# A causal convolution computed by parity of tokens, group sums in float32r, and the first tokens laid out by part

## The chip, the cores and the metric

The kernel runs on one core of a Trainium2 chip. The metric is the device time of one execution in microseconds, the median of several runs.

## The reference, cut to what matters

One decoder layer, 2048 tokens of 1024 channels, all in float32. This case touches the first of its stages (phase A): the normalisation of x, the projection `w_in`, and the two causal convolutions over tokens, above all the wide one:

```python
u = conv_val * jax.nn.sigmoid(conv_gate)
u = causal_depthwise_conv(u, conv_w[layer], conv_b[layer])      # width 31, 512 channels
uf = u.astype(jnp.float32).reshape(B, S, N_CONV_GROUPS, CONV_GROUP_DIM)
mu_c = jnp.mean(uf, axis=-1, keepdims=True)                     # over 128 channels of a group
var_c = jnp.mean(jnp.square(uf - mu_c), axis=-1, keepdims=True)
uf = ((uf - mu_c) * lax.rsqrt(var_c + EPS)).reshape(B, S, D_CONV)
uf = uf * conv_norm_w[layer] + conv_norm_b[layer]
y_conv = jax.nn.silu(uf)
```

Queries and keys pass a convolution of width 4 and a silu. Behind it come the mLSTM, the output projection, two norms and the MLP; none of them is changed.

## The kernel before, in words

Channels lie on partitions and tokens along the free axis. Every large product is made of three float32r matmuls, high by high, high by low and low by high part of both operands. A high part is a rounding copy on ScalarE (ACT), a low part a subtraction on VectorE (DVE).

Phase A goes in 96 **slots** (SLOTS). A slot is one PSUM bank of output, 24 matmuls of 128x512 or 48 of half the width (kinds v and o). PE, ACT and DVE each have their own program, written slot by slot: for every slot `s` ACT evacuates the bank when PE has ended the slot (`evacuate`, semaphore proj), and then does the other steps that belong to `s`, in the order of the code; DVE does the same for its own. Nothing is reordered at run time, so a step that waits holds up everything that stands behind it on its engine.

The wide convolution comes in 8 **units** (4 groups of 128 channels, 2 halves of 1024 tokens). `glu` writes a unit's input into `u_buf`, a ring of three. On DVE a unit is 30 steps of `tap`: taps 2 to 30, each a multiply-add over 1024 tokens, alternately into `c_buf` and `c_odd`, and one addition of the two. Taps 0 and 1 are made on ACT by `first_tap` (into c_buf, of which there are two) and `second_tap` (into c_odd, of which there is one). `tap_plan` decides how many steps DVE does in each slot: a slot has room 100, a tap costs TAP_COST 23, a convolution of queries or keys 76, a split of weights 22. CONV_END[u] is the slot in which a unit ends. By it the norm's steps are placed: at CONV_END + 1 PE sums over channels by float32 matmuls with a matrix of ones (`group_sum`, L501), at + 2 DVE centers, at + 3 ACT squares, at + 4 PE sums again, at + 5 ACT makes the reciprocal root, at + 6 DVE multiplies, at + 7 ACT applies silu and stores the result.

The convolutions of width 4 (`first_tap_qk` on ACT L649, `convolve_qk` on DVE L852, `silu_qk` on ACT L655 with a store) stand at the slots of Q_AT: 10, 13, 15, 17, then 33, 35, 37, 39, 49, 51, 53, 55, 73, 75, 77, 79. ACT does `silu_qk` of slot s - 2 and then `first_tap_qk` of slot s, both on the one buffer `qout`, so the first tap waits until the store of the convolution before has landed.

At the start SP loads x of the first 512 tokens in two parts of 256 (`load_first`), the parameters, and the first weight tiles. PE makes warming matmuls (`warm`), then sums of squares of x in float32 (L388), while ACT and DVE square and split.

## Time and profile before

| | |
|---|---|
| time, median of 3 runs | 2086.41 us (2086.11 to 2086.6) |
| the profiled execution, time | 2085.33 us |
| its span, first to last instruction | 2083.5 us |
| granted TensorE clock, mean | 0.998 |
| PE busy | 2067.1 us (99%), 10031 matmuls |
| DVE, ACT, POOL busy | 1446.1, 912.1, 417.2 us |
| HBM traffic | 225.58 MB read, 111.21 MB written |

Durations are those of one execution by the hardware's profiler. A record's duration holds the latency of the engine too, so where instructions follow each other closely, the distance of their starts is what each takes. A bracket behind a row of a timeline gives the idle time before it and who ended it. A float32 matmul shows as two records, one for each pass.

### The profile page before, as it was taken

How to read it: one execution, taken by the hardware profiler on the slowest of the kernel's cores; microseconds unless marked ns; L12 is line 12 of the kernel's file. 1: busy time of each engine (PE TensorE's matmuls, PEld its weight loads, DVE VectorE, ACT ScalarE, POOL GpSimd, SP SyncE). 2: the span in 40 equal slices, each digit the busy share in tenths (PEclk: the TensorE clock that was granted, in tenths of full speed). 3: DMA queues.
4: the chain of work that ended last, by engine and by line, in shares of the span. 5: the costliest groups of instructions: out<-in, count | busy, mean ns of one | idle time of the engine just before them, and what ended most of it. 6: DMA issues, size and time to landing. Idle time of an engine off the chain costs nothing. (4 is left out here: it accounts for less than half of the span.)

```text
span 2083.5 us, 26901 instructions
## 1 busy us (share of the span) xinstructions
PE 2067.1 (99%) x10031; PEld 1734.2 (83%) x10031; DVE 1446.1 (69%) x1993; ACT 912.1 (44%) x1557; POOL 417.2 (20%) x252
## 2 busy tenths in 40 slices
PE   9999999999999999999999999999999999999998
PEld 8897878878788888788888888888788888888887
DVE  6897999989567777886666976666563536624285
ACT  6632434343454445754555654455331313313163
POOL 0000000000002323352332333232353134400012
PEclk9999999999999999999999999999999999999999
DMA  5121212113656875765446755545756455543376
GB/s 204 32 87 47 70 41 81 51 32 105 199 177 195 266 235 171 266 192 167 137 142 191 236 171 156 167 150 189 245 210 259 154 193 202 174 169 126 138 257 218
DMA packets 254144, 338.55 MB, mean 162 GB/s; under 512 B 11584, under 2 KB 195648, under 8 KB 240192
## 3 DMA queue, kind: packets, MB, share of 16 engines
q1 hardware_dynamic: 221376, 315.80, 45.6%
q10 hardware_dynamic: 32384, 20.98, 3.2%
q8 instruction: 81, 1.33, 0.3%
q14 instruction: 47, 0.39, 0.1%
q0 software_dynamic: 256, 0.07, 0.0%
HBM read 225.58 MB, written 111.21 MB: 162 GB/s over the span
## 5 line engine op out<-in xcount | busy, mean ns | idle before, releaser
L1978 PE MATMUL psum<-x_hi,w_hi_P 128*128 128x512 f32 x896 | 349.8, 390 | 3.8 <-DVE x_lo L1922 2.4
L2198 PE MATMUL psum<-w_hi,hid_hi 128*128 128x512 f32 x896 | 348.8, 389 | 1.9 <-DVE hid_lo L2074 1.9
L1978 PE MATMUL psum<-x_lo,w_hi_P 128*128 128x512 f32 x896 | 349.1, 390 | 0.0
L1978 PE MATMUL psum<-x_hi,w_lo_P 128*128 128x512 f32 x896 | 349.1, 390 | 0.0
L2198 PE MATMUL psum<-w_hi,hid_lo 128*128 128x512 f32 x896 | 348.6, 389 | 0.0
L2198 PE MATMUL psum<-w_lo,hid_hi 128*128 128x512 f32 x896 | 348.6, 389 | 0.0
L2074 DVE TENSOR_TENSOR hid_lo<-hid_raw,hid_hi 128x1024 fp32r<-128x1024 f32 x112 | 174.4, 1593 | 211.4 <-ACT hid_hi L2069 211.4
L1891 POOL TENSOR_TENSOR w_raw<-w_raw 128x512 f32<-128x512 f32 x128 | 184.9, 1467 | 395.3 <-DVE w_lo_P L1904 345.8
L2069 ACT ACTIVATE hid_hi<-hid_raw 128x1024 fp32r<-128x1024 f32 x112 | 112.9, 1051 | 343.4 <-DMA hid_raw<-scratch_hid 343.3
L1904 DVE TENSOR_TENSOR w_lo_P<-w_raw,w_hi_P 128x512 fp32r<-128x512 f32 x224 | 184.1, 834 | 98.1 <-ACT w_hi_P L1900 95.5
L1900 ACT ACTIVATE w_hi_P<-w_raw 128x512 fp32r<-128x512 f32 x224 | 136.0, 626 | 236.8 <-PE psum L1978 227.2
L1978 PEld LDWEIGHTS psum<-x_hi,w_hi_P 128*128 128x128 f32 x896 | 168.4, 188 | 40.4 <-issue 5.9
L2198 PEld LDWEIGHTS psum<-w_hi,hid_hi 128*128 128x128 f32 x896 | 168.2, 188 | 37.5 <-issue 2.7
L1978 PEld LDWEIGHTS psum<-x_hi,w_lo_P 128*128 128x128 f32 x896 | 168.5, 188 | 35.5
L1978 PEld LDWEIGHTS psum<-x_lo,w_hi_P 128*128 128x128 f32 x896 | 168.6, 188 | 34.7
L2198 PEld LDWEIGHTS psum<-w_hi,hid_lo 128*128 128x128 f32 x896 | 168.2, 188 | 35.0
L2198 PEld LDWEIGHTS psum<-w_lo,hid_hi 128*128 128x128 f32 x896 | 168.2, 188 | 34.9
L2030 POOL TENSOR_TENSOR w_raw<-w_raw,w_grain 128x1024 f32<-128x1024 f32 x48 | 137.9, 2888 | 224.5 <-DMA w_grain<-in_w 224.5
L841 DVE SCALAR_TENSOR_TENSOR c_buf<-u_buf,par_a,c_buf 128x1024 f32<-128x1024 f32 x120 | 153.2, 1276 | 0.0
L841 DVE SCALAR_TENSOR_TENSOR c_odd<-u_buf,par_a,c_odd 128x1024 f32<-128x1024 f32 x112 | 142.9, 1276 | 5.2 <-ACT c_odd L638 5.2
L404 PE MATMUL psum<-big_hi,w_hi 128*128 128x512 f32 (+1 forms) x288 | 109.0, 378 | 0.8 <-DVE big_lo L795 0.7
L2323 DVE TENSOR_TENSOR c<-c,psum 128x512 f32<-128x512 f32 x96 | 65.4, 681 | 61.9 <-PE psum L1978 61.9
(284 smaller groups left out, 3820.0 us busy)
## 6 DMA issues: line engine op xcount, KB each, us to landing
scratch_hid<-stage SPq DMA_DIRECT2D x224, 256.0 KB, 3.7
hid_raw<-scratch_hid SPq DMA_DIRECT2D x56, 1024.0 KB, 4.9
w_raw<-in_w SPq DMA_DIRECT2D x52, 1024.0 KB, 5.0
w_grain<-in_w SPq DMA_DIRECT2D x48, 512.0 KB, 5.3
x_raw<-scratch_h2s SPq DMA_DIRECT2D x14, 1024.0 KB, 8.4
w_raw<-in_w_in SPq DMA_DIRECT2D x22, 512.0 KB, 3.6
scratch_h2s<-h2s SPq DMA_DIRECT2D x8, 1280.0 KB, 10.1
scratch_qk<-qout ACTq DMA_DIRECT2D x16, 512.0 KB, 3.3
```

The lines of the kernel that those rows point to most:

```text
L404: mm = nc.tensor.matmul(out, a, b, start=kt == 0 and i == 0, stop=kt == KT - 1 and i == 2)
L841: nc.vector.scalar_tensor_tensor(out=out, in0=u_buf[:, u % U_RING, k:k + HALF], scalar=par[:, CONV_W + g * CW + k:CONV_W + g * CW + k + 1] ...
L1891: nc.gpsimd.tensor_tensor(raw_1(op), raw_1(a), raw_1(b), ALU.subtract).then_inc(sem["w1_t"], 1)
L1900: nc.scalar.activation(w1_hi[op][:], raw_1(op), ACT.Copy).then_inc(sem["w1_hi"], 1)
L1904: nc.vector.tensor_tensor(w1_lo[op][:], raw_1(op), w1_hi[op][:].bitcast(F32), ALU.subtract).then_inc(sem["w1_lo"], 1)
L1978: mm = nc.tensor.matmul(psum[:, bank_1(op, g), :], l, r, start=kt == 0 and i == 0, stop=kt == 3 and i == 2)
L2030: nc.gpsimd.tensor_tensor(part, part, grain[:, n % 2], alu).then_inc(sem["w2_t"], 1)
L2069: nc.scalar.activation(hid_hi[n % HID_RING][:, half_fps(h)], hid_raw[n % HID_RING][:, half_fps(h)], ACT.Copy).then_inc(sem["hid_hi"], 1)
L2074: nc.vector.tensor_tensor(hid_lo[n % HID_RING][:, half_fps(h)], hid_raw[n % HID_RING][:, half_fps(h)], hid_hi[n % HID_RING][:, half_fps(h) ...
L2198: mm = nc.tensor.matmul(psum[:, bank, :], l, r, start=f == 0 and k == 0, stop=f == NFP - 1 and k == 2)
L2323: nc.vector.tensor_tensor(out[:], a[:], ps1(op, g), ALU.add).then_inc(sem["gather"], 1)
```

## The change

1. **The convolution by parity.** `u_buf` holds the even and the odd tokens of a unit in two halves. With E and O the input's even and odd tokens, the even outputs are A + B (A: even taps on one half, B: odd taps on the other), the odd outputs are M - A' - B, where M takes sums of neighbouring inputs (`add_pairs`, step S) with sums of neighbouring weights (`add_weights`). A unit is 48 steps on about 512 elements instead of 30 on 1024: S, 15 of A, 14 of B, 15 of M, and E, T, O, which combine them. Three first taps on ACT (`first_taps` for A and B, `pair_tap` for M) replace two. A and B lie in one buffer `ab_buf`; `first_taps` stands at slot max(CONV_START - 1, glu_end, CONV_END of the unit before) and waits for that unit's T and O. A step costs STEP_COST 11.5 in the plan.
2. **The norm's sums in float32r.** ACT makes a high part of the unit (AT_HIGH) and of its square, DVE the low parts (AT_LOW, AT_SQUARE_LOW), and PE adds high and low by float32r matmuls: 8 per unit instead of 4 float32 ones. The steps stand at other slots (UNIT_AT), and the low part of a unit goes to DVE behind the taps and q/k convolution of slot CONV_END + 1.
3. **The first 512 tokens.** They lie in DRAM as `x_first`, by part; the first part comes in two DMAs by halves of channels, with w0 before them and the parameters behind them. ACT and DVE square alternate pairs, both split w0 first. 18 warming matmuls stand where 30 stood.

The silu writes tokens back in order (stride 2). The diff, cut to its core:

```diff
-DVE_TAPS = CW - 1
+EVEN, ODD = (CW + 1) // 2, CW // 2
+UH = HALF // 2
+UX = UH + EVEN
 
 
 def tiles_of(slot):
...
+AT_HIGH, AT_SUM_HIGH, AT_LOW, AT_SUM_LOW, AT_CENTER, AT_SQUARE, AT_SQUARE_LOW, AT_VAR, AT_RSTD, AT_NORM, AT_SILU = (
+    "high", "sum_high", "low", "sum_low", "center", "square", "square_low", "var", "rstd", "norm", "silu")
+UNIT_AT = {AT_HIGH: 0, AT_SUM_HIGH: 1, AT_LOW: 1, AT_SUM_LOW: 2, AT_CENTER: 2, AT_SQUARE: 3, AT_SQUARE_LOW: 3,
+           AT_VAR: 4, AT_RSTD: 5, AT_NORM: 6, AT_SILU: 7}
+LAST_UNIT_AT = {AT_HIGH: 0, AT_SUM_HIGH: 1, AT_LOW: 1, AT_SUM_LOW: 2, AT_CENTER: 2, AT_SQUARE: 2, AT_SQUARE_LOW: 2,
+                AT_VAR: 3, AT_RSTD: 3, AT_NORM: 3, AT_SILU: 3}
+LN_SUMS = 6
 FIRST_LOOP = 11
-TAP_COST = 23
+STEP_COST = 11.5
...
+WARM, WARM_MORE = 18, 8
...
+def unit_steps():
+
+    out = [("S", 0)]
+    for j in range(1, EVEN):
+        out += [("A", j)] + ([("B", j)] if j < ODD else []) + ([("M", j - 1)] if j > 1 else [])
+    return out + [("E", 0), ("M", EVEN - 1), ("T", 0), ("O", 0)]
...
-            room -= 22 * sum(out[s - AT_NORM] >= DVE_TAPS * (u + 1) > out[s - AT_NORM - 1] for u in range(N_UNITS))
-        ends = [min(i for i in range(s) if out[i] >= DVE_TAPS * (u + 1)) for u in range(n // DVE_TAPS)]
+            for at in (AT_LOW, AT_CENTER, AT_SQUARE_LOW, AT_NORM):
+                room -= 22 * sum(out[s - UNIT_AT[at]] >= N_STEPS * (u + 1) > out[s - UNIT_AT[at] - 1] for u in range(N_UNITS))
...
-        more = max(0, min(ready - n, room // TAP_COST))
+                ready = min(ready, N_STEPS * u)
+        more = max(0, min(ready - n, int(room // STEP_COST)))
...
-FIRST_TAP = [max(min(s for s in range(N_SLOTS) if TAPS[s] > DVE_TAPS * u) - 1, glu_end(u)) for u in range(N_UNITS)]
-CONV_END = [min(s for s in range(N_SLOTS) if TAPS[s] >= DVE_TAPS * (u + 1)) for u in range(N_UNITS)]
-
-SECOND_TAP = [max(FIRST_TAP[u], CONV_END[u - 1] if u else 0) for u in range(N_UNITS)]
+CONV_START = [min(s for s in range(N_SLOTS) if TAPS[s] > N_STEPS * u) for u in range(N_UNITS)]
+CONV_END = [min(s for s in range(N_SLOTS) if TAPS[s] >= N_STEPS * (u + 1)) for u in range(N_UNITS)]
+
+FIRST_TAP = [max(CONV_START[u] - 1, glu_end(u), CONV_END[u - 1] if u else 0) for u in range(N_UNITS)]
+
+PAIR_TAP = [max(FIRST_TAP[u], CONV_START[u]) for u in range(N_UNITS)]
...
+        ab_buf = sb("ab_buf", [P, 2 * UH + 1])
+        a_sum, b_sum = ab_buf[:, 0:UH + 1], ab_buf[:, UH + 1:2 * UH + 1]
...
-                sp.dma_start(big["raw"][:, :, at], dram["xt"][:, :, at]).then_inc(sem["x_in"][part], 16)
+                for half, landed in enumerate((sem["x_in"][0], sem["x_head"])) if part == 0 else ():
+                    kt = slice(half * KT // 2, (half + 1) * KT // 2)
+                    sp.dma_start(big["raw"][:, kt, at], dram["x_first"][0, :, kt]).then_inc(landed, 16)
+                if part == 1:
+                    sp.dma_start(big["raw"][:, :, at], dram["x_first"][1]).then_inc(sem["x_in"][1], 16)
...
+            load_w(0)
             load_first(0)
             sp.dma_start(par[:], dram["params_a"]).then_inc(sem["par_a"], 16)
-            load_w(0)
...
-                elif kt < KT // 2:
-                    pe.wait_ge(sem["x_sq"], kt // 2 + 1)
                 else:
-                    pe.wait_ge(sem["x_sq_dve"], (kt - KT // 2) // 2 + 1)
+                    pe.wait_ge(sem["x_sq" if kt // 2 % 2 == 0 else "x_sq_dve"], kt // 4 + 1)
...
-            def group_sum(src, b):
-                nc.tensor.matmul(psum[:, 6 + b, :], ones[:], src[:, b * TB:(b + 1) * TB],
-                                 start=True, stop=True).then_inc(sem["ln_sum"], 1)
+            def group_sum(src, b, start, stop):
+                return nc.tensor.matmul(psum[:, 6 + b, :], ones_r[:], src[:, b * TB:(b + 1) * TB], start=start, stop=stop)
...
-                for u in units_at(s, AT_MEAN):
-                    pe.wait_ge(sem["tap"], DVE_TAPS * (u + 1))
+                for u in units_at(s, AT_SUM_HIGH):
+                    pe.wait_ge(sem["ln_act"], 3 * u + 1)
                     if u == 0:
                         pe.wait_ge(sem["x_rstd"], NTB + 1)
                     else:
                         pe.wait_ge(sem["c_rstd"], 2 * u)
                     for b in range(2):
-                        group_sum(c_buf[:, u % 2], b)
+                        group_sum(high_part(u), b, True, False).then_inc(sem["ln_sum"], 1)
+                for u in units_at(s, AT_SUM_LOW):
+                    pe.wait_ge(sem["ln_dve"], 3 * u + 1)
+                    for b in range(2):
+                        group_sum(high_part(u), b, False, True).then_inc(sem["ln_sum"], 1)
                 for u in units_at(s, AT_VAR):
-                    pe.wait_ge(sem["c_sq"], u + 1)
+                    pe.wait_ge(sem["ln_act"], 3 * u + 3)
+                    pe.wait_ge(sem["ln_dve"], 3 * u + 3)
                     for b in range(2):
-                        group_sum(rstd, b)
+                        group_sum(high_part(u), b, True, False)
+                        group_sum(square_low, b, False, True).then_inc(sem["ln_sum"], 1)
...
-            def first_tap(u):
+            def first_taps(u):
                 g = u // 2
                 act.wait_ge(sem["evac"]["dve"], 2 * (u + 1))
                 act.wait_ge(sem["u_head"], u + 1)
-                if u >= 2:
-                    act.wait_ge(sem["c_out"][u % 2], 16 * (u // 2))
-                nc.scalar.activation(c_buf[:, u % 2], u_buf[:, u % U_RING, 0:HALF], ACT.Identity,
+                if u >= 1:
+                    act.wait_ge(sem["tap"], step_done(u - 1, "T"))
+                nc.scalar.activation(a_sum, u_halves(u)[:, 0, 0:UH + 1], ACT.Identity,
                                      scale=par[:, CONV_W + g * CW:CONV_W + g * CW + 1],
                                      bias=par[:, CONV_B + g:CONV_B + g + 1]).then_inc(sem["tap0"], 1)
-
-            def second_tap(u):
+                if u >= 1:
+                    act.wait_ge(sem["tap"], step_done(u - 1, "O"))
+                nc.scalar.activation(b_sum, u_halves(u)[:, 1, 0:UH], ACT.Copy,
+                                     scale=par[:, CONV_W + g * CW + 1:CONV_W + g * CW + 2]).then_inc(sem["tap0"], 1)
+
+            def pair_tap(u):
                 g = u // 2
-                if u >= 1:
-                    act.wait_ge(sem["tap"], DVE_TAPS * u)
-                nc.scalar.activation(c_odd[:], u_buf[:, u % U_RING, 1:1 + HALF], ACT.Copy,
-                                     scale=par[:, CONV_W + g * CW + 1:CONV_W + g * CW + 2]).then_inc(sem["tap0"], 1)
+                act.wait_ge(sem["tap"], step_done(u, "S"))
+                if u >= 2:
+                    act.wait_ge(sem["c_silu"], u - 1)
+                nc.scalar.activation(m_sum(u), u_pairs(u)[:, 0:UH], ACT.Identity, scale=pair_weight(g, 0),
+                                     bias=pairs[:, H * EVEN + g:H * EVEN + g + 1]).then_inc(sem["tap0"], 1)
...
+            split_w(0)
+            for q in (0, 2):
+                square_pair(q, 0)
+            split_w(1)
             act.wait_ge(sem["par_a"], 16)
...
+                for u in units_at(s, AT_HIGH):
+                    act.wait_ge(sem["tap"], step_done(u, "O"))
+                    nc.scalar.activation(high_part(u), c_buf[:, u % 2], ACT.Copy).then_inc(sem["ln_act"], 1)
                 for u in units_at(s, AT_SQUARE):
-                    act.wait_ge(sem["c_center"], u + 1)
+                    act.wait_ge(sem["ln_dve"], 3 * u + 2)
                     if u >= 1:
                         act.wait_ge(sem["c_norm"], u)
-                    nc.scalar.activation(rstd[:], c_buf[:, u % 2], ACT.Square).then_inc(sem["c_sq"], 1)
+                        act.wait_ge(sem["c_out"][(u - 1) % 2], 16 * ((u - 1) // 2 + 1))
+                    nc.scalar.activation(rstd[:], c_buf[:, u % 2], ACT.Square).then_inc(sem["ln_act"], 1)
+                    act.wait_ge(sem["ln_act"], 3 * u + 2)
+                    act.wait_ge(sem["ln_sum"], LN_SUMS * u + 4)
+                    nc.scalar.activation(high_part(u), rstd[:], ACT.Copy).then_inc(sem["ln_act"], 1)
...
+                    nc.scalar.activation(c_tokens(u)[:].rearrange("p (n a) -> p a n", a=2),
+                                         c_buf[:, u % 2].rearrange("p (a n) -> p a n", a=2), ACT.Silu,
+                                         scale=par[:, CN_W + g:CN_W + g + 1],
...
-                        first_tap(u)
-                    if SECOND_TAP[u] == s:
-                        second_tap(u)
+                        first_taps(u)
+                    if PAIR_TAP[u] == s:
+                        pair_tap(u)
...
+                at = ODD + (tb % 2) * TB // 2
                 if tb % 2 == 0 and u >= U_RING:
-                    dve.wait_ge(sem["tap"], DVE_TAPS * (u - U_RING + 1))
+                    dve.wait_ge(sem["ln_sum"], LN_SUMS * (u - U_RING + 1))
...
+                gate, val = (a.rearrange("p (n a) -> p a n", a=2) for a in (th[:, (th_uses(s) - 1) % 2, :], psum[:, banks_of(s)[0], :]))
+                nc.vector.scalar_tensor_tensor(out=u_halves(u)[:, :, at:at + TB // 2], in0=gate, scalar=1.0, in1=val,
+                                               op0=ALU.add, op1=ALU.mult).then_inc(sem["evac"]["dve"], 1)
...
+            def even_tap(u, j):
+
+                g = u // 2
+                if j == 1:
+                    dve.wait_ge(sem["tap0"], 3 * u + 1)
...
+            def pair_tap(u, j):
+
+                if j == 1:
+                    dve.wait_ge(sem["tap0"], 3 * u + 3)
+                else:
+                    dve.wait_ge(sem["tap"], step_done(u, "M", j - 1))
+                nc.vector.scalar_tensor_tensor(out=m_sum(u), in0=u_pairs(u)[:, j:j + UH], scalar=pair_weight(u // 2, j),
+                                               in1=m_sum(u), op0=ALU.mult, op1=ALU.add).then_inc(sem["tap"], 1)
...
+            def even_tokens(u):
+
+                dve.wait_ge(sem["tap"], step_done(u, "A", EVEN - 1))
+                nc.vector.tensor_tensor(c_buf[:, u % 2, 0:UH], a_sum[:, 0:UH], b_sum, ALU.add).then_inc(sem["tap"], 1)
+
+            def both_sums(u):
+
+                dve.wait_ge(sem["tap"], step_done(u, "E"))
+                nc.vector.tensor_tensor(b_sum, a_sum[:, 1:UH + 1], b_sum, ALU.add).then_inc(sem["tap"], 1)
+
+            def odd_tokens(u):
+
+                dve.wait_ge(sem["tap"], step_done(u, "T"))
+                nc.vector.tensor_tensor(m_sum(u), m_sum(u), b_sum, ALU.subtract).then_inc(sem["tap"], 1)
...
+            add_weights()
             for s in range(N_SLOTS):
                 if SLOTS[s][0] == "val" and s >= EARLY_EVACS:
                     glu(s)
                 for n in range(TAPS[s - 1] if s else 0, TAPS[s]):
-                    tap(n)
+                    conv_step(n)
                 for j, half in convs_at(s - 1):
                     convolve_qk(j, half)
+                for u in units_at(s, AT_LOW):
+                    dve.wait_ge(sem["ln_sum"], LN_SUMS * u + 2)
+                    nc.vector.tensor_tensor(high_part(u), c_buf[:, u % 2], high_part(u).bitcast(F32),
+                                            ALU.subtract).then_inc(sem["ln_dve"], 1)
                 for u in units_at(s, AT_CENTER):
-                    dve.wait_ge(sem["ln_sum"], 4 * u + 2)
+                    dve.wait_ge(sem["ln_sum"], LN_SUMS * u + 4)
                     nc.vector.scalar_tensor_tensor(out=c_buf[:, u % 2], in0=ln_ps, scalar=-1.0 / P, in1=c_buf[:, u % 2],
-                                                   op0=ALU.mult, op1=ALU.add).then_inc(sem["c_center"], 1)
+                                                   op0=ALU.mult, op1=ALU.add).then_inc(sem["ln_dve"], 1)
...
+                for u in units_at(s, AT_SQUARE_LOW):
+                    dve.wait_ge(sem["ln_act"], 3 * u + 3)
+                    nc.vector.tensor_tensor(square_low[:], rstd[:], high_part(u).bitcast(F32),
+                                            ALU.subtract).then_inc(sem["ln_dve"], 1)
...
+        "x_first": np.ascontiguousarray(x[0, :TB].T.reshape(KT, P, 2, PART).transpose(2, 1, 0, 3)),
+        "xt": np.ascontiguousarray(x[0, TB:].T.reshape(KT, P, S - TB).transpose(1, 0, 2)),
```

## Rows read from the trace of the kernel before

**Rows 1.** The page: busy us of each engine with its share; granted clock.

```profile
PE 2067.1 (99%) x10031; PEld 1734.2 (83%) x10031; DVE 1446.1 (69%) x1993; ACT 912.1 (44%) x1557; POOL 417.2 (20%) x252
...
PEclk9999999999999999999999999999999999999999
```

**Rows 2.** The waits of PE: who waited for whom, us in total, times, longest.

```profile
PE psum L501 <- DVE c_buf L838: 1.1, 3, 0.8
```

**Rows 3.** Groups of PE: shapes, count | busy us, mean ns | idle before.

```profile
L501 PE MATMUL psum<-c_buf,ones 128*128 128x512 f32 x32 | 15.3, 602 | 1.1 <-DVE c_buf L838 1.1
```

**Rows 4.** Timeline of PE at the first group sum: start us, us, what, count.

```profile
157.74 1.88 PE L501 MATMUL psum<-c_buf,ones 128*128 128x512 f32 x4
159.05 0.80 PE L404 MATMUL psum<-big_hi,w_hi 128*128 128x512 f32 x1
159.68 0.39 PE L404 MATMUL psum<-big_lo,w_hi 128*128 128x512 f32 x1
```

**Rows 5.** Timeline of ACT, two evacuations that end slots 13 and 14.

```profile
100.65 0.60 ACT L596 ACTIVATE qraw<-psum 128x512 f32<-128x512 f32 x1 [0.81 <-PE psum L404]
...
106.09 0.60 ACT L606 ACTIVATE th<-psum 128x512 f32<-128x512 f32 x1 [0.89 <-PE psum L404]
```

**Rows 6.** Timeline of DVE in slots 37 and 38.

```profile
241.44 1.22 DVE L808 TENSOR_TENSOR w_lo<-w_raw,w_hi 128x1024 fp32r<-128x1024 f32 x1
242.58 1.28 DVE L841 SCALAR_TENSOR_TENSOR c_buf<-u_buf,par_a,c_buf 128x1024 f32<-128x1024 f32 x1
243.77 1.28 DVE L841 SCALAR_TENSOR_TENSOR c_odd<-u_buf,par_a,c_odd 128x1024 f32<-128x1024 f32 x1
...
248.56 3.92 DVE L852 SCALAR_TENSOR_TENSOR qout<-qraw,par_a,qout 128x1024 f32<-128x1024 f32 x3
252.40 0.16 DVE L855 COPY qraw<-qraw 128x3 f32<-128x3 f32 x1
```

**Rows 7.** Timeline of DVE, operations on 512 elements in the normalisation of x.

```profile
62.36 0.75 DVE L800 SCALAR_TENSOR_TENSOR x_raw<-x_raw,par_a,rstd_a 128x512 f32<-128x512 f32 x1
63.02 0.68 DVE L795 TENSOR_TENSOR h_lo<-x_raw,h_hi 128x512 fp32r<-128x512 f32 x1
63.62 0.74 DVE L800 SCALAR_TENSOR_TENSOR x_raw<-x_raw,par_a,rstd_a 128x512 f32<-128x512 f32 x1
```

**Rows 8.** Timeline of ACT in slot 37.

```profile
242.08 1.14 ACT L655 ACTIVATE qout<-qout,par_a 128x1024 f32<-128x1024 f32 x1
...
246.32 1.16 ACT L649 ACTIVATE qout<-qraw,par_a 128x1024 f32<-128x1024 f32 x1 [3.10 <-DMA scratch_qk<-qout]
```

**Rows 9.** The waits of all engines from 90 to 565 us.

```profile
DVE c_odd L841 <- ACT c_odd L638: 5.2, 2, 3.0
```

**Rows 10.** Stretches of 1 us: busy of PE, PEld, DVE, ACT, POOL; clock; DMA.

```profile
854.00:855.00 1.00, 1.00 (x4) 0.86 (x5) 1.00 (x1) 1.00 (x2) 0.92 (x1) 0.86 1.06 389
...
856.00:857.00 1.00, 0.99 (x3) 0.79 (x3) 1.00 (x2) 1.00 (x2) 0.00 (x0) 0.50 1.05 387
...
858.00:859.00 1.00, 1.00 (x6) 0.83 (x5) 1.00 (x2) 0.00 (x0) 0.00 (x0) 0.94 1.06 363
```

**Rows 11.** Timeline of all engines at the start.

```profile
0.99 8.76 PE L377 MATMUL psum<-ones 128*128 128x128 f32 x60 [0.99 <-POOL ones L368]
...
9.19 1.16 ACT L551 ACTIVATE c_buf<-big_raw 128x512 f32<-128x512 f32 x2 [7.16 <-DMA par_a<-in_params_a]
...
11.58 2.56 DVE L808 TENSOR_TENSOR w_lo<-w_raw,w_hi 128x1024 fp32r<-128x1024 f32 x2 [0.83 <-ACT w_hi L581]
11.82 1.06 ACT L581 ACTIVATE w_hi<-w_raw 128x1024 fp32r<-128x1024 f32 x1 [0.27 <-DMA w_raw<-in_w_in]
...
14.59 0.88 DVE L800 SCALAR_TENSOR_TENSOR big_raw<-big_raw,par_a,rstd_a 128x256 f32<-128x256 f32 x2 [0.45 <-ACT rstd_a L571]
...
16.12 0.35 PE L404 MATMUL psum<-big_hi,w_hi 128*128 128x256 f32 x1 [0.75 <-DVE big_lo L795]
```

More of the change, by code:

```diff
@@ L549, in square_pair @@
             def square_pair(q, part):
-                act.wait_ge(sem["x_in"][part], 16)
+                if part == 0 and q >= KT // 4:
+                    act.wait_ge(sem["x_head"], 16)
+                else:
+                    act.wait_ge(sem["x_in"][part], 16)
                 nc.scalar.activation(x_sq_pair(q, part), x_pair(q, part), ACT.Square).then_inc(sem["x_sq"], 1)
@@ new lines, in glu @@
+                gate, val = (a.rearrange("p (n a) -> p a n", a=2) for a in (th[:, (th_uses(s) - 1) % 2, :], psum[:, banks_of(s)[0], :]))
[5 more added lines that the diff above has]
+                    dve.wait_ge(sem["tap0"], 3 * u + 1)
+                else:
+                    dve.wait_ge(sem["tap"], step_done(u, "A", j - 1))
+                nc.vector.scalar_tensor_tensor(out=a_sum, in0=u_halves(u)[:, 0, j:j + UH + 1],
+                                               scalar=par[:, CONV_W + g * CW + 2 * j:CONV_W + g * CW + 2 * j + 1],
+                                               in1=a_sum, op0=ALU.mult, op1=ALU.add).then_inc(sem["tap"], 1)
@@ new lines, in odd_tap @@
+            def odd_tap(u, j):
+                g = u // 2
+                if j == 1:
+                    dve.wait_ge(sem["tap0"], 3 * u + 2)
+                else:
+                    dve.wait_ge(sem["tap"], step_done(u, "B", j - 1))
+                nc.vector.scalar_tensor_tensor(out=b_sum, in0=u_halves(u)[:, 1, j:j + UH],
+                                               scalar=par[:, CONV_W + g * CW + 2 * j + 1:CONV_W + g * CW + 2 * j + 2],
+                                               in1=b_sum, op0=ALU.mult, op1=ALU.add).then_inc(sem["tap"], 1)
@@ new lines, in conv_step @@
+            def conv_step(n):
+                u = n // N_STEPS
+                kind, j = STEPS[n % N_STEPS]
+                if kind == "S":
+                    add_pairs(u)
+                elif kind == "A":
+                    even_tap(u, j)
+                elif kind == "B":
+                    odd_tap(u, j)
+                elif kind == "M":
+                    pair_tap(u, j)
+                elif kind == "E":
+                    even_tokens(u)
+                elif kind == "T":
+                    both_sums(u)
+                else:
+                    odd_tokens(u)
@@ new lines, in add_weights @@
+            def add_weights():
+                taps = par[:, CONV_W:CONV_W + H * CW].rearrange("p (g k) -> p g k", g=H)
+                sums = pairs[:, 0:H * EVEN].rearrange("p (g j) -> p g j", g=H)
+                nc.vector.tensor_tensor(sums[:, :, 0:ODD], taps[:, :, 0:CW - 1:2], taps[:, :, 1:CW - 1:2], ALU.add)
+                nc.vector.tensor_copy(sums[:, :, ODD:EVEN], taps[:, :, CW - 1:CW])
+                link(nc.vector.tensor_scalar(pairs[:, H * EVEN:H * EVEN + H], par[:, CONV_B:CONV_B + H], 2.0, None, ALU.mult))
@@ L858, in vector @@
             nc.vector.memset(eps[:], EPS).then_inc(sem["eps_a"], 1)
+            split_w(0)
+            for q in (1, 3):
+                square_pair(q)
             dve.wait_ge(sem["par_a"], 16)
@@ L1238, in load_first @@
                     sp.dma_start(o_c[c], dram["o"][c]).then_inc(sem["chunk_in"][c], 16)
-                sp.wait_ge(sem["tap"], DVE_TAPS * N_UNITS)
+                sp.wait_ge(sem["tap"], N_STEPS * N_UNITS)
                 sp.wait_ge(sem["rows_out"], 2 * H * 16)
@@ L2468, in semaphores @@
     named["scores_in"] = named["w_raw"][:C_RING]
+    named["x_head"] = named["wpost"]
     named["evac"] = {e: ctx.enter_context(nc.semaphore(f"evac_{e}")) for e in ("act", "dve")}
```

105 lines of the change are left out of this document (55 added, 50 removed).

## Prediction

> **What bounds the kernel now.** I read the page's busy table and clock line first, then the list of waits on PE, then the first 560 us engine by engine. PE is busy for 2067.1 of 2083.5 us at full clock [rows 1], so time can only be won where PE has less to do or waits less. What it waits is small: in the convolution stage the sums of the norm waited for the last tap 1.1 us in three places [rows 2]. The change touches only the stage from 0 to about 560 us (phase A). After it PE runs on without a long gap, so a shift at its end arrives whole at the end of the kernel. A slot of 24 matmuls takes 5.44 us (the evacuations of two slots stand at 100.65 and 106.09, both just released by PE [rows 5]), 0.227 us for one 128x512 float32r matmul.
>
> **The sums of the norm.** Each float32 matmul of L501 runs as two passes [rows 3]. Four passes begin at 157.74 and the matmul behind them ends its own turn at 159.68, one pace of 0.23 before which PE was free, so two matmuls take 1.71 us, 0.857 each [rows 4]. There are 32 of them (8 units, 2 sums, 2 banks): 27.4 us on PE's path. The new code does 8 float32r matmuls per unit, 64 at 0.227: 14.5 us. That is -12.9 us. Bounds: if each cost its whole record of about 0.39 us [rows 4] it would be 25.0 and the gain 2.4; between other matmuls they overlap as L404's do, so I take 0.227. Below 0.227 no row goes.
>
> **The convolution on DVE.** Before, a unit is 29 multiply-adds of 1024, 1.20 us from start to start, and one addition: about 35.9 us [rows 6]. After, it is 44 multiply-adds of 512 or 513 and 4 additions. A multiply-add of 512 by the same form takes 0.66 us from start to start, an addition or subtraction 0.60 [rows 7]. So 44 x 0.664 + 4 x 0.61 + 0.2 for two that wait for their predecessor = 31.9 us. Two new subtractions of 1024 for the low parts cost 1.15 each (the same form begins at 241.44 and the next instruction at 242.58 [rows 6]): 34.2 us, 1.7 less than before. DVE is not the bound by itself. But the planner (tap_plan) now charges 11.5 for a step where it charged 23 for a tap. In us per unit of plan that was 1.20/23 = 0.052 and is now 0.664/11.5 = 0.058, while a slot's 100 units last 5.44 us: 0.054. DVE had 4% in hand and is now 6% over where the plan fills a slot. It falls behind the slots.
>
> By the Trainium skill, "VectorE: DVE Perf Modes", section on the TRN2 errata, a VectorE operation pays a fixed term of about 150 cycles whatever its size, which speaks against cutting one operation in two. An estimate from that page's figures is (150 + 512)/0.96 GHz = 0.69 us each, so 44 would take 30.4 us instead of 29.2, if nothing of it overlaps with the neighbour. The trace has the neighbours overlapping, and the sum goes by the trace.
>
> **The order on ACT, which is the point.** One buffer (ab_buf) now serves both sums, so the first taps of a unit wait for the end of the unit before, and they stand in ACT's program at slot CONV_END[u-1], behind the evacuation, the high copy, silu_qk and first_tap_qk of that slot. Working the planner out with the new constants, the units end in slots 20, 27, 37, 46, 55, 63, 73, 83 (before: 22, 29, 41, 49, 60, 68, 79, 87). Slots 37 and 55 also hold a q/k convolution whose first tap waits for the store of the one before. That row exists: silu at 242.08, its store, and the first tap only at 246.32, 3.1 us of idle ACT [rows 8]. The same conflict already showed once small: DVE waited for the second tap, 5.2 us in two places [rows 9].
>
> Unit 2, from the end of slot 35 (t = 0; the convolutions of slots 35 and 37 are (2,1) and (3,0)). ACT: evacuation 0.5, silu 1.15, store 3.07, first tap 1.15. DVE: q/k convolution 3.83 (248.56 to 252.40 [rows 6]), w_lo 1.15, last five steps of unit 2 3.3. The unit is done at 14.2. Then ACT: high copy 1.06 (a copy of this form takes 1.06 [rows 11]), silu 1.15, store 3.07, first tap of (3,0) 1.06, first tap of unit 3 0.69. DVE, in order: three steps 2.0, convolution (3,0) 3.83, and only then the low part of unit 2, 1.23: 28.3. PE has slots 36 to 39 and two sums, 22.2, and then waits for that low part: 6.1 us. What is queued behind it is every later matmul.
>
> Unit 4 is alike in slots 53 to 57. Laying the three programs one behind the other with the same durations, from slot 12 on, the last step of unit 4 comes 2.3 us after the end of slot 56, the high copy follows, and PE waits 3.4 us for it. From the unit's end the chain to its low part is again 14.0 us, PE has 1.15 + 0.46 + 5.7 (slot 57) = 7.3 before it: 6.7 us more, 5.1 if PE lost 1.7 us to its clock meanwhile. (Laid out in the same way, the kernel before has its unit ends within 1 us of the trace as far as unit 5, and its stage end 1.2 us early.) Smaller waits of the same lag, at units 1, 3, 6 and 7 (0.4, 1.6, 3.0 and 0.1), and 0.5 at slot 54: 5.6; against them 1.1 us of PE waits of before go [rows 2]. +4.5.
>
> **The clock.** After PE had stood idle for 2.2 us its granted clock was 0.86 in the microsecond from 854, 0.50 from 856, the lower of its two levels (1.2 against 2.4 GHz), and 0.94 in the one from 858 [rows 10]. With 855 and 857 like 856 that is 3.2 us at half pace, about 1.7 us lost. The waits of 6.1, 3.4 and 5.1 us are all longer: 3 x 1.7 = +5.1. The largest wait at unit 6, 2.2 us, may bring 0 or 1.7; I take 0 to hold the sum to the three sure ones.
>
> **Start.** Now squares start at 9.19, released by par_a (x, the DMA before it, is there by then), DVE ends the low parts of both weight tiles at 14.14 and the first normalisation starts at 14.59, the first matmul at 16.12 [rows 11]. The new order puts w0 first, both halves of x, par_a, then w1. The bytes ahead of w1's end are the same, and w1 must still be split on ACT (1.06) and DVE (1.15 to 1.25), which stand before the first normalisation. With w1 where it was (its ACT split began at 11.82) that ends at 14.1, 0.5 us better. If 4 KB runs instead of 1 KB ones bring w1 1.4 us sooner, 1.9 better. Against it, 18 warming matmuls are 36 passes and end at 6.3 to 7.1 (60 passes end at 9.75 [rows 11]; at the mean pace of 0.143 the 24 fewer take 3.4 us away, and a faster late pace only 2.7), so PE is idle some 2 to 3 us before x, and at the lower clock up to 1.7 us can be lost. Value -0.5, ends -1.9 and +1.7. The squares by part, the other loads and the semaphore are off the path or change nothing.
>
> **At nothing.** ACT gains two copies of 1024 per unit (2.1 us) and loses 0.3 by the shorter first taps; it lies idle for PE most of a slot, except where named above, where the copy is in the chain. Stride-2 reads and writes in the gate's product (16, 0.61 each now) and in silu (8): no row has such a stride; from 0 to twice as long, 10 us more of DVE in all, off PE's path unless DVE lags there, 0 to +2. I take 0, since both work on 4-byte elements one by one. add_weights is three small operations before the loop.
>
> **Sum against the profiled execution.** It took 2085.3 us with a span of 2083.5; the median of three is 2086.4, so I count differences and set them on the median. -12.9 (sums) + 6.1 + 3.4 + 5.1 (waits at units 2 and 4) + 4.5 (lag elsewhere, net) + 5.1 (clock) - 0.5 (start) = +10.8, which I round down to +10 since the lag waits partly replace each other. 2096 us.
>
> **Rivals.** (a) Faster: DVE and ACT keep up. The deciding point is unit 2's last step: if it is out when slot 37 ends, 3.3 us sooner than I sum, the chain behind it (0.5 for the evacuation and 14.1) meets PE's 11.3 and leaves 3.3 us, at unit 4 2.7, with no fall of the clock: 2086.4 - 12.9 - 0.5 + 6.0 - 1.1 = 2078. For it: DVE's total work falls. Against it: the landing of 3.1 us and the lag per full slot. (b) No change: the waits of 6.1, 3.4 and 5.1 come, but the clock holds and no lag adds: 2086.4 - 12.9 - 0.5 + 14.6 - 1.1 = 2086.5. Against it, the clock fell at 2.2 us. (c) Slower still: stride or step pace puts DVE 3% further behind (0.68 to 0.70 per step), each wait grows by 0.3 to 1, unit 6 brings a fourth fall of the clock and the start loses 1.7: +8, 2104. (d) The sums don't run as hoped, at 0.39 each: the gain is 2.4, the result 2106 with all else; little speaks for it.
>
> **Chances.** Forecast 2096 (2090.6 to 2101): 0.57. (a) 0.17, (b) 0.13, (c) 0.10, (d) 0.03. Range 2079 to 2106: it leaves out half of (a) and little above. About 0.2% (4 us) is what a measurement of this kernel can tell from no change. Faster 0.17, within it 0.13, slower 0.70.
>
> **What would show it.** Right: DVE idle about 6 us before the first even tap of units 3 and 5, released by ACT's first taps; PE waiting before sums of low parts for DVE subtractions at about 250 and 365 us, with the clock at 0.50 behind them; 64 sum records some 0.227 apart; unit length on DVE near 32 us of work. Wrong: DVE's steps below 0.64 from start to start, PE's waits in the stage below 8 us in all, or the stage ending before 560 us.

## The result, and the profile after

The changed kernel takes 2097.55 us (median; 2096.98 to 2099.38) against 2086.4 for the kernel before, run beside it: ratio 1.0052, 95% interval 1.0037 to 1.0067. That is 11.2 us slower; 10 us slower was forecast.

The page of the changed kernel, busy time and slices, answers to [rows 1]:

```profile
PE 2057.5 (98%) x10007; PEld 1734.5 (83%) x10007; DVE 1436.3 (69%) x2164; ACT 929.0 (44%) x1581; POOL 418.9 (20%) x252
## 2 busy tenths in 40 slices
PE   9999898999999999899999999999999999999998
```

PE has 9.6 us less to do in a span 12.2 us longer (2095.7). The first two eights lie at about 210 to 260 and 310 to 370 us (a slice is 52 us). The list of PE's waits says who made it stand, and answers to [rows 2]:

```profile
PE psum L558 <- DVE u_high L1038: 17.2, 4, 7.4
...
PE psum L558 <- ACT u_high L770: 3.2, 1, 3.2
...
PE psum L558 <- DVE square_low L1046: 0.9, 2, 0.5
```

L558 is a sum of the norm (`group_sum`), L1038 the subtraction that makes a low part, L770 the copy that makes a high part, L1046 the low part of the square. Sums waited 1.1 us before; now 21.8. In the timeline of PE, these are the four largest gaps:

```profile
253.93 1.22 PE L558 MATMUL psum<-u_high,ones 128*128 128x512 f32 x2 [6.98 <-DVE u_high L1038]
...
358.03 0.73 PE L558 MATMUL psum<-u_high,ones 128*128 128x512 f32 x2 [3.22 <-ACT u_high L770]
...
371.94 1.22 PE L558 MATMUL psum<-u_high,ones 128*128 128x512 f32 x2 [7.44 <-DVE u_high L1038]
...
482.23 0.90 PE L558 MATMUL psum<-u_high,ones 128*128 128x512 f32 x2 [1.79 <-DVE u_high L1038]
```

They are the low sum of unit 2, the high and the low sum of unit 4, and the low sum of unit 6: forecast at 6.1, 3.4, 5.1 and 2.2.

How the first of them comes about stands in the timelines of ACT and DVE. Slot 35 was evacuated at 224.71. ACT (L770 high copy, L725 silu, L728 its store, L719 first tap of the q/k convolution, L695 first tap of the wide one):

```profile
239.66 1.06 ACT L770 ACTIVATE u_high<-c_buf 128x1024 fp32r<-128x1024 f32 x1 [3.48 <-DVE c_buf L965]
240.63 1.13 ACT L725 ACTIVATE qout<-qout,par_a 128x1024 f32<-128x1024 f32 x1
241.79 0.37 ACTq L728 DMA_DIRECT2D scratch_qk<-qout  x1
244.86 1.15 ACT L719 ACTIVATE qout<-qraw,par_a 128x1024 f32<-128x1024 f32 x1 [3.10 <-DMA scratch_qk<-qout]
245.92 0.80 ACT L695 ACTIVATE ab_buf<-u_buf,par_a 128x513 f32<-128x513 f32 x1
```

DVE (L965 ends unit 2, L920 and L931 taps of unit 3, L1000 the q/k convolution, L1038 the low part of unit 2):

```profile
238.94 0.69 DVE L965 TENSOR_TENSOR c_buf<-c_buf,ab_buf 128x512 f32<-128x512 f32 x1
239.55 0.70 DVE L949 TENSOR_TENSOR u_pairs<-u_buf 128x527 f32<-128x527 f32 x1
246.76 0.76 DVE L920 SCALAR_TENSOR_TENSOR ab_buf<-u_buf,par_a,ab_buf 128x513 f32<-128x513 f32 x1 [6.51 <-ACT ab_buf L695]
247.43 0.75 DVE L931 SCALAR_TENSOR_TENSOR ab_buf<-u_buf,par_a,ab_buf 128x512 f32<-128x512 f32 x1
248.09 0.75 DVE L920 SCALAR_TENSOR_TENSOR ab_buf<-u_buf,par_a,ab_buf 128x513 f32<-128x513 f32 x1
248.75 3.92 DVE L1000 SCALAR_TENSOR_TENSOR qout<-qraw,par_a,qout 128x1024 f32<-128x1024 f32 x3
...
252.66 1.22 DVE L1038 TENSOR_TENSOR u_high<-c_buf,u_high 128x1024 fp32r<-128x1024 f32 x1
```

From the end of unit 2 (239.63) the chain to PE's start is: copy, silu, store 3.10, two first taps, three steps, the q/k convolution, and at last the subtraction: 14.3 us. PE had ended its work at 246.95.

The clock behind these waits, in stretches of 1 us (span of the stretch, PE's busy us, clock, DMA's share, GB/s):

```profile
254.00:255.00 1.00, 1.00 (x3) 0.50 0.09 27
...
257.00:258.00 1.00, 1.00 (x5) 0.82 0.00 0
...
359.00:360.00 1.00, 1.00 (x10) 1.00 0.10 23
...
374.00:375.00 1.00, 1.00 (x7) 0.50 0.50 150
...
484.00:485.00 1.00, 1.00 (x3) 0.50 1.12 336
```

After 6.98 and 7.44 us of idleness PE works at the lower level, as in [rows 10]; after the 1.79 us at 480 too (the clock was still 1.00 when PE went on and 0.50 one microsecond later), but not after the 3.22 us at 355.

**The account.** The evacuation of slot 91, the last of the stage, begins at 578.30; before at 565.74, so 12.6 us later. Start: -3.0 (the first matmul at 13.14, [rows 11] had 16.12). Sums: 64 at 0.231 to 0.238 from start to start, 15.0 us for 27.4, -12.4. PE's gaps in the stage add up to 23.2 against 1.9: +21.3. Clock: three falls of 1.6, 2.2 and 1.7 (the time of the matmuls behind the wait, less what as many take at full clock): +5.5. Together +11.4; 1.2 us I can't place. Behind slot 91 little changes (+12.2 at the end of the span).

### The profile page after: what moved, and what is told of

The parts are those of the page before. It is cut to its first block and busy times, and to the rows that moved or that the text cites. A ratio compares the mean times of both kernels' runs of the same rounds, so it can differ in the third digit from the quotient of the medians.

```text
span 2095.7 us, 27079 instructions
## 1 busy us (share of the span) xinstructions
PE 2057.5 (98%) x10007; PEld 1734.5 (83%) x10007; DVE 1436.3 (69%) x2164; ACT 929.0 (44%) x1581; POOL 418.9 (20%) x252
## 3 DMA queue, kind: packets, MB, share of 16 engines
q8 instruction: 81, 1.33, 0.3%
## 5 line engine op out<-in xcount | busy, mean ns | idle before, releaser
L2231 DVE TENSOR_TENSOR hid_lo<-hid_raw,hid_hi 128x1024 fp32r<-128x1024 f32 x112 | 179.2, 1636 | 199.5 <-ACT hid_hi L2226 199.4
L461 PE MATMUL psum<-big_lo,w_hi 128*128 128x512 f32 (+1 forms) x288 | 106.4, 370 | 0.0
L461 PE MATMUL psum<-big_hi,w_lo 128*128 128x512 f32 (+1 forms) x288 | 106.2, 369 | 0.0
```

Source lines behind the costliest of these rows:

```text
L461: mm = nc.tensor.matmul(out, a, b, start=kt == 0 and i == 0, stop=kt == KT - 1 and i == 2)
L2231: nc.vector.tensor_tensor(hid_lo[n % HID_RING][:, half_fps(h)], hid_raw[n % HID_RING][:, half_fps(h)], hid_hi[n % HID_RING][:, half_fps(h) ...
```

## The experiments

Three theories stood for the waits. A: the first taps stand too late on ACT, behind the store of the q/k convolution, and starve DVE. B: the low part stands on DVE behind a q/k convolution. C: DVE and ACT are behind the plan throughout, since a step is charged too little; order matters only because of that.

**e1: only the first taps moved, ahead of silu and first tap of q/k.**

```diff
+                for u in range(N_UNITS):
+                    if FIRST_TAP[u] == s:
+                        first_taps(u)
+                    if PAIR_TAP[u] == s:
+                        pair_tap(u)
                 for j, half in convs_at(s - 2):
                     silu_qk(j, half)
                 for j, half in convs_at(s):
                     first_tap_qk(j, half)
```

> The changed kernel with one thing moved: on ACT the first taps of a unit stand ahead of silu_qk and first_tap_qk of the same slot. Theory A (the prediction's: the place of the first taps on ACT starves DVE, and so delays the low part): DVE's waits for ab_buf fall from 17.3 us to under 7, the waits of PE for the low parts of units 2 and 4 (7.0 and 7.4 us) to under 1.5 each, the clock stays up, time 2078 to 2084. Theory B (the low part stands behind the q/k convolution, whose own first tap waits for the store): DVE's idle time only moves from the even tap to the convolution, the two waits shrink by about 1 us each, time 2092 to 2097. Theory C (DVE is behind its plan): no change beyond 1 us, 2096 to 2098.

2094.26 us, ratio 1.0038 (1.0023 to 1.0053). The waits of PE:

```profile
PE psum L558 <- DVE u_high L1038: 11.8, 4, 6.2
```

And of all engines from 90 to 575 us:

```profile
DVE qout L1000 <- ACT qout L719: 20.6, 7, 6.9
...
DVE ab_buf L920 <- ACT ab_buf L695: 4.9, 4, 1.2
```

In the changed kernel DVE waited 17.3 us for first taps and 12.5 for those of q/k; now 4.9 and 20.6. Two thirds of the wait went over to the next step of the queue that hangs on the same store. Only 3.3 us came back: A alone falls. The time lies where B was expected, and above the 1 us that C allowed.

**e2: only the low parts moved, ahead of the q/k convolution on DVE.**

```diff
+                for u in units_at(s, AT_LOW):
+                    ...
                 for j, half in convs_at(s - 1):
                     convolve_qk(j, half)
-                for u in units_at(s, AT_LOW):
-                    ...
```

> The changed kernel with one thing moved: on DVE the low part of a unit stands ahead of the q/k convolution of its slot. Theory A: DVE is still idle 6 to 7 us at the first even tap, three steps and the low part follow: the waits at units 2 and 4 fall by 3.8 (the convolution's length) to about 3, but a fall of the clock may stay; time 2088 to 2094. Theory B: the waits go to under 1 us, time 2078 to 2084. Theory C: no change beyond 1 us for unit 4's wait on its high part, which stays at 3.2.

2092.26 us, 1.0032 (1.0019 to 1.0045). PE:

```profile
PE psum L558 <- DVE u_high L1036: 6.0, 3, 3.1
PE psum L558 <- DVE square_low L1046: 6.0, 5, 2.0
```

The wait for low parts falls from 17.2 to 6.0, that for low parts of squares rises from 0.9 to 6.0. B alone would have given 2078 to 2084 and falls as well. Here the time lies where A was expected, so each of the two is refuted by its own experiment.

**e3: both moved.**

> Both moves of the two kernels before. Theories A and B together (each of them alone holds the low part back): no wait at the low parts of units 2, 4 and 6, yet PE waits about 3 us for the squares of units 2, 4 or 6, since DVE reaches the subtraction of the square late behind the convolution; what is left is 3.2 at unit 4's high part and small ones, stage end 10 us sooner, time 2085 to 2089. Theory C: a time above 2092.

2089.11 us, 1.0014 (1.0004 to 1.0024), just above what was expected. PE:

```profile
PE psum L558 <- DVE square_low L1046: 9.2, 5, 4.6
```

The waits of the low sums are gone but for one of 1.0, and those of the squares' sums are 9.2. With both orders mended, the norm's next step is late: DVE has a backlog, and whatever stands last in it makes PE wait. The backlog speaks for C, but C as it was put on record (above 2092) is missed: the two moves give back 8.4 us. A and B together come close to time and waits.

**e4: only the charge for a step.** `STEP_COST` 13.2 for 11.5; units end in slots 21, 29, 40, 49, 60, 67, 79, 87.

> The changed kernel with STEP_COST 13.2 instead of 11.5, so that a step of 0.664 us is planned at 0.0503 us per unit of plan, as a tap was before (0.052). Units then end in slots 21, 29, 40, 49, 60, 67, 79, 87. Theory C (DVE is behind its plan, and this alone makes the waits): PE's waits in the stage fall from 23 us to under 7, unit 6 (slot 79, again a q/k slot) keeps 4 to 5; time 2074 to 2078. Theories A and B alone: the waits follow the q/k slots: 49 and 79 are such slots, so two waits of 5 to 7 us stay, with the clock's fall; time 2086 to 2092.

2091.53 us, 1.0023 (1.0012 to 1.0033). The waits of the sums are 6.3 us instead of 21.8 and slot 91 is evacuated at 563.67, 14.6 us sooner than in the changed kernel. Two waits of 1.9 and 2.3 us on ACT (L1261 at 417, L1268 at 451) are new, so PE's waits in the stage are 10.4 us, where C expected under 7. And at its end, in the timeline of PE:

```profile
569.31 2.05 PE L1546 MATMUL psum<-q_t,k_t 128*128 128x128 f32 x8 [7.60 <-DMA yc_c<-scratch_yc]
```

With unit 7 ending in slot 87 its norm and silu end at 562.4, its store is issued then, and the first scores of the next stage wait for its data, with the clock at 0.50 until 572. So the charge does bring the sums' waits down, but most of the gain is lost at the stage's end, which the 2074 to 2078 expected of C left out.

A second thing changes with the charge. In the changed kernel three units end in a slot that also holds a q/k convolution: 2, 4 and 6 (slots 37, 55, 73), and 19.4 of the 21.8 us are their waits. Here units 3 and 6 do (slots 49 and 79), and the waits are theirs, 1.1 and 5.1. Whether the sums wait less because DVE has more room, or because fewer units end beside a q/k convolution, this run doesn't tell apart.

**e5: the kernel before with the new start alone.** The loads, the order of squares and splits, 18 warming matmuls.

> The kernel before with the start of the changed one alone: x_first by part and halves, w0 first, squares by alternate pairs, 18 warming matmuls. The changed kernel's first projection matmul stands at 13.14 us against 16.12. If PE carries this through the stage (theory), the time is 3.0 us below that of the kernel before. Rival: the later loads of x or the last tap, which DVE ends just in time, take it back: 0 to 1.5 us below.

2084.83 us, 0.9995 (0.9986 to 1.0004): no change that can be told. But the ten times lie in two groups, five from 2082.56 to 2083.87 and four from 2087.87 to 2088.70, with one between (2085.79); the kernel before ranged from 2084.64 to 2089.20 beside them. The trace is of the slowest, 2088.70, and shows how the gain can be lost, not what the median does; what the fast ones do, no trace shows. In it the first matmul is at 14.12, 2.0 us sooner; slot after slot stays 2.0 us sooner, until slot 87:

```profile
538.47 2.14 PE L503 MATMUL psum<-c_buf,ones 128*128 128x512 f32 x3 [2.14 <-DVE c_buf L846]
```

PE is now 2 us ahead of unit 7's last tap (it waited 0.8 for it before), and its clock falls behind the wait. Slot 91 of this execution ends 1.0 us later than in the kernel before.

**e6: the changed kernel with float32 sums.** No high or low parts; convolution by parity and start as in the changed kernel.

> The changed kernel with the norm's sums by float32 matmuls again (4 per unit, no high and low parts; centering, squaring and the rest at the changed kernel's slots), so convolution by parity and the new start alone. Theory B (the low part behind the q/k convolution makes most of the waits): 18 us of waits and the clock's falls go, 12.4 us of matmuls come back: 2082 to 2087. Theory C (DVE is behind its plan, whatever the sums are): waits of 2 to 4 us for the last step at units 2, 4 and 6 stay, 2088 to 2094.

2085.79 us, 0.9996 (0.9987 to 1.0005). The sums wait 2.1 us, once, for unit 4's last step, and the clock falls behind it (the trace is of the slowest execution, 2088.18). So the convolution by parity and the start leave the time where it was, and the float32r sums, which take 12.4 us from PE, are what costs 11.8 us (2097.55 - 2085.79), by the high and low parts that they need, in the queues as they stand. The time lies where B was expected, and below C's 2088 to 2094: the charge of 11.5 and the slots in which units end are those of the changed kernel, and yet almost no wait is left. But this is no clean test of C. `tap_plan` still keeps 22 of a slot's 100 for each of the two low parts that DVE no longer makes, 44 per unit, and the 48 steps are charged 48 x 0.7 = 34 too little: here DVE is not over its plan. The low charge without that spare room was not tried.

**e7: the clock held.** 26 matmuls on data that is at hand, into the bank of the next slot, ahead of the low sums of units 2 and 4; all else as in the changed kernel.

```diff
                 for u in units_at(s, AT_SUM_LOW):
+                    if u in (2, 4):
+                        ...
+                        for _ in range(26):
+                            nc.tensor.matmul(psum[:, bank, :], ones_r[:], tokens(h_hi, 0, 0, TB), start=True, stop=True)
                     pe.wait_ge(sem["ln_dve"], 3 * u + 1)
```

> The changed kernel with 26 more float32r matmuls (5.9 us) on PE ahead of the wait for the low part of units 2 and 4, into the bank of the next slot, which writes it anew: they fill the waits of 7.0 and 7.4 us, so that PE is idle for 1 to 2 us only. Theory: what PE loses at granted clock 0.50 behind these two waits is on the path; time 3 to 4 us below the changed kernel, 2093.5 to 2094.5. Rival: the next waits for DVE take it back, as PE comes to them sooner: within 1 us of 2097.5.

2094.09 us, 1.0036 (1.0022 to 1.0049); slot 91 is evacuated at 573.97, 4.3 us sooner. The granted clock behind unit 2's wait was 1.00 (254 to 257), and there was no wait left at unit 4's low sum. But two other waits of nearly the same length as before turned out the other way:

```profile
357.28 0.73 PE L558 MATMUL psum<-u_high,ones 128*128 128x512 f32 x2 [3.17 <-ACT u_high L777]
...
479.26 0.73 PE L558 MATMUL psum<-u_high,ones 128*128 128x512 f32 x2 [1.81 <-DVE u_high L1045]
```

```profile
359.00:360.00 1.00, 1.00 (x7) 0.50 0.82 247
...
481.00:482.00 1.00, 1.00 (x6) 1.00 1.13 339
```

The clock fell at unit 4's high sum, where it had held, and held at unit 6, where it had fallen. The two falls that the matmuls were to prevent had been read as 1.6 + 2.2 us; 3.5 us came back in the median of four executions, which lie from 2092.43 to 2096.91. That agrees in size with what was read and shows that the clock's cost is on the path; how much of it each fall makes, the two exchanged falls and the spread don't let one say.

**e8: planned anew.** `STEP_COST` 13.0, low sum and center one slot later, square and its low part, sum and root likewise (the last unit and the norm's last two steps unchanged), and both moves of e3.

```diff
-UNIT_AT = {AT_HIGH: 0, AT_SUM_HIGH: 1, AT_LOW: 1, AT_SUM_LOW: 2, AT_CENTER: 2, AT_SQUARE: 3, AT_SQUARE_LOW: 3,
-           AT_VAR: 4, AT_RSTD: 5, AT_NORM: 6, AT_SILU: 7}
+UNIT_AT = {AT_HIGH: 0, AT_SUM_HIGH: 1, AT_LOW: 1, AT_SUM_LOW: 3, AT_CENTER: 3, AT_SQUARE: 4, AT_SQUARE_LOW: 4,
+           AT_VAR: 5, AT_RSTD: 6, AT_NORM: 6, AT_SILU: 7}
-STEP_COST = 11.5
+STEP_COST = 13.0
```

> All three causes treated: STEP_COST 13.0, first taps ahead of the q/k steps on ACT, low part ahead of the q/k convolution on DVE, and the low sum, centering, square and variance sum one slot later (3, 3, 4, 5; reciprocal root and normalisation both at 6). Units end in slots 21, 29, 40, 48, 59, 67, 77, 86. Theories B and C together: PE's waits in the stage 3 to 6 us, no fall of the clock, stage end at 551 to 556 us: 2070 to 2077, faster than the kernel before. Theory A or C alone: waits of 5 us or more stay at one of the q/k slots (77), 2080 to 2086.

2077.61 us, 0.9955 (0.9941 to 0.9968): faster than both kernels, 8.4 us below the one before, and 0.6 above what was expected. PE:

```profile
PE psum L558 <- DVE square_low L1046: 3.8, 3, 2.5
...
PE psum L537 <- ACT th L680: 2.8, 1, 2.8
```

The units end in slots 21, 29, 40, 48, 59, 67, 77, 86: the last one a slot sooner than in e4, and no wait before the first scores remains. The clock was expected to hold; it fell behind the waits of 2.47 (unit 6's squares) and 2.80 us. Slot 91 is evacuated at 558.81, 19.5 us sooner than in the changed kernel.

**e9: the plan of e8 without the two moves.**

> The replanned kernel (a step charged 13 units, the norm's later steps one slot later) without its two moves: first taps behind the q/k convolution on ACT and low parts behind it on DVE, as in the changed kernel. If the plan alone keeps DVE in step (theory C), the two moves are worth at most 1 us: 2077 to 2079. If the order inside a slot still costs where a q/k convolution falls beside a unit's end (theories A and B), PE waits some 4 us more in all before sums of low parts and before squares: 2080 to 2083.

2078.72 us, 0.9964 (0.9951 to 0.9977). The medians of e8 and e9 differ by 1.1 us and their intervals overlap: with this plan no worth of the two moves can be told, as C expects. The same two moves were worth 8.4 in the changed kernel (e3). So the order inside a slot costs under one plan and not under the other. The new plan differs in three things at once: the charge, the later slots of the norm, and that only one unit (6, slot 77) still ends beside a q/k convolution; it has the longest wait of a sum left, 3.4 of 5.1 us. Which of the three does most was not tried.

**e10: e8 with float32 sums.**

> The replanned kernel with float32 sums of the norm, two per sum instead of four float32r ones, and no high or low parts (four operations of ACT and DVE less per unit). The sums alone cost PE 32 x 0.857 - 64 x 0.231 = 12.6 us more. If the float32r sums are worth that once nothing waits for their operands, the waits of the replanned kernel (8.7 us) shrink to some 3 and the time is 2083 to 2087. If the extra operations of the high and low parts take back what PE wins, as in the changed kernel against the one with float32 sums (2097.5 against 2085.8), it is 2078 or below.

2082.75 us, 0.9984 (0.9975 to 0.9993), just under the first case. In the stage PE waits for no sum at all. So the float32r sums are worth 5.1 us with a plan that makes room for them (2082.75 - 2077.61), 12.4 less 4.1 us of waits for high and low parts, 0.8 more for an evacuation (2.8 against 2.0), and the clock, which fell behind two of e8's waits and not here. And without them the convolution by parity, the start and the new plan with both moves are together worth 3.6 us against the kernel before (2086.32 beside this run).

**e11: e5 with the last unit's norm one slot later.**

> The kernel before with the new start alone, and the norm's steps of the last unit one slot later, so that PE doesn't wait for its last tap at slot 87. If the 2.0 us that the start wins were lost only by that wait and the clock behind it, the gain stays: 2083 to 2084.2 against 2086.0 (ratio 0.9986 to 0.9991). If the later end of unit 7 holds up the first scores instead (the load of yc stands behind it), the gain is gone or turned round: 2085 to 2090.

2084.47 us, 0.9992 (0.9983 to 1.0000): between the two cases. The wait for the tap is gone and PE stays 2.5 us ahead until slot 90. Then:

```profile
557.65 0.47 PE L482 MATMUL psum<-w_hi,h_hi 128*128 128x512 f32 x1 [1.93 <-ACT th L620]
```

ACT did the silu of unit 7 (554.35) and loaded a table (555.61 to 556.9) before it evacuated the bank that PE wants, and the clock was 0.50 from 559 to 562. The evacuation of slot 91 is 0.7 us sooner than before. The same wait is the 2.8 us of e8 and e9. At the end of the stage the last unit's chain is a bound of its own, on DVE, then on ACT, then on its store; whether a later silu would take it off was not tried.

## Why the prediction was right, point by point

**The sums:** -12.9 forecast, -12.4 measured. The pace is 0.231 to 0.238, not 0.227.

**The convolution on DVE:** steps 0.664 apart (225.50, 226.16, 226.82), as summed. That DVE is over its plan where slots are full is a part of the cause: in units of the plan a step is 0.664 / 5.44 x 100 = 12.2, and a charge of 13.2 alone took the waits of the sums from 21.8 to 6.3 us (e4). The high and low parts are what PE waits for: without them, and with their room on DVE left free, 2.1 us of waits remain (e6).

**"The order on ACT, which is the point":** the chain was right, the emphasis was not. Unit 2's last step came 14.9 us after the end of slot 35 (14.2 forecast), the low part 14.3 behind it (14.1), the wait 6.98 (6.1). DVE's idle time before the first even tap was 6.5 us at unit 3 and 7.3 at unit 5, forecast as about 6. But the queue has three such places, the first taps on ACT, the low part on DVE and the low part of the squares on DVE. e1 and e2 take away one each, and e3 two, and the wait moves on to the next.

**Unit 4:** 3.22 (3.4 forecast) and 7.44 (5.1). The step that was off is the subtraction of 1.7 us for a clock that PE would lose behind the first wait: it didn't fall there. Without that the sum gave 6.7; the store took 3.93 instead of 3.07 to land, which is most of the rest.

**Lag elsewhere:** +4.5 net forecast. The other gaps are 0.41, 0.98, 0.48, 0.59, 1.79, 0.52 and 0.78: 5.6 us, less 1.9 of before: +3.7. Unit 6 was forecast at 3.0 in all and gave 1.8.

**The clock:** +5.1 forecast, 5.5 measured, but not at all three places named: it fell at unit 2, at the low sum of unit 4 and at unit 6, of which the last had been left at nothing. By the Trainium skill, "TensorE: Matmul & The Clock Gate", section "HAM oscillation — how this bites in real kernels", each wait for data between bursts of matmuls can put TensorE back on the lower clock, and the remedy is to keep it from waiting. e7 agrees: with 26 matmuls in place of most of unit 2's wait the clock behind it was 1.00 where it had been 0.50. But not every wait did it: the clock held after 3.22 us.

**The start:** -0.5 forecast, bounds -1.9 and +1.7; measured -3.0, outside the bounds. The step that failed is the time at which the loads are there. For w1 I allowed 1.4 us sooner; in the timeline of ACT its split (the third row here) began at 9.08 against 11.82, 2.7 us sooner. And x, which I had left off the path, came sooner too, its halves squared from 6.04 and 7.54 against 9.19:

```profile
4.59 1.06 ACT L646 ACTIVATE w_hi<-w_raw 128x1024 fp32r<-128x1024 f32 x1 [2.56 <-DMA w_raw<-in_w_in]
...
6.04 0.63 ACT L616 ACTIVATE c_buf<-big_raw 128x512 f32<-128x512 f32 x1 [0.39 <-DMA big_raw<-in_x_first]
...
9.08 1.06 ACT L646 ACTIVATE w_hi<-w_raw 128x1024 fp32r<-128x1024 f32 x1 [0.91 <-DMA w_raw<-in_w_in]
```

It is the squares' side that ended last: the first normalisation (11.60) waited 0.21 us for ACT's reciprocal root, which had waited for PE's sums of squares and not for w1. The first half of x is there before the warming matmuls end (7.07), so the gap and the cold clock that made the other bound never came. The eleven other traces with this start have the first matmuls 2.0 to 2.9 us sooner than before, so up to 1 us of the -3.0 is chance.

**At nothing.** This held. The gate's product took 0.684 us with the stride as without, the silu 1.33 for 1.24.

**The rivals.** (a), faster at 2078, is refuted: its condition (unit 2 ending in time) isn't met. That e8 and e9 measure about 2078 is no confirmation of its sum, since they put the units' ends and the norm's steps in other slots and have the start at its full 2.4 to 2.8 us. (b) missed the clock. (c) is refuted by the pace of 0.664, though the fall at unit 6 that it named did come; (d) by the pace of the sums.

The mechanism was right; that +10 came so close to +11.2 is in part luck, for two errors nearly cancel: the start gave 2.5 us more than forecast, and the waits of units 2 and 4 took 3.0 us more.

## What to carry to other kernels

Before work is taken from the busiest engine by giving others more, count what they have left in each slot at the pace of the trace, and charge a hand-written plan with no less than that pace: 0.664 us were charged as 11.5 of 100 where they are 12.2 (13.0 and 13.2 were tried, 12.2 not), and a change that takes 12.4 us from PE made the kernel 11.2 slower. Where moving one waiting step moves most of the wait to the next, the queue as a whole is late: sorting it gave back 8.4 us (e3), changing its schedule 18.8 (e9). A stage's last unit has no slots behind it to hide in: look at its chain by itself, on each engine and up to its store.

## What the runs showed of the hardware

**When the clock falls.** It fell after idle times of 1.79 and 1.93 us (unit 6 of the changed kernel, e11) and not after 3.22 (its unit 4). In e7 the same two places gave the opposite: it fell after 3.17 us and held after 1.81. In e9 and e8 PE waits 2.80 us for the same evacuation; behind it the matmuls start 0.23 apart in one and 0.43 in the other. The second matmuls of both:

```profile
553.39 0.40 PE L537 MATMUL psum<-w_lo,h_hi 128*128 128x512 f32 x1
553.63 0.40 PE L537 MATMUL psum<-w_hi,h_lo 128*128 128x512 f32 x1
```

```profile
552.25 0.63 PE L537 MATMUL psum<-w_lo,h_hi 128*128 128x512 f32 x1
552.68 0.63 PE L537 MATMUL psum<-w_hi,h_lo 128*128 128x512 f32 x1
```

So the length of a wait alone doesn't settle it, and the cost of a wait of 2 to 3 us has to be given with both ends, 0 and the 1.6 to 2.2 us of the falls measured here. What decides was not tried.

**Loads at the start.** With w0 ahead of x and x in two DMAs of longer runs, w0 and half of x are there by 6.04 us and the other half by 7.54, where x and the parameters took until 9.19 [rows 11] and w0 until 10.49 (the start of its split in the timeline of ACT). Which of order and layout does it was not told apart.
